# Hybrid SSD and pooling decoder step: the sample's state addition on GpSimd instead of VectorE, and its square sums two pool products later

## The reference

```python
def step(s, inp):                      # per sample token: decay the state, add the outer product
    dec, st = inp
    return s * dec[..., None, None] + st, s
...
y = y_diag + y_off                     # y_t = S_t C_t for the sample
y = y + d_skip * xs
y = y * silu(z)
yg = yg * rsqrt(mean(yg * yg) + EPS)   # per group of 512 channels
...
merged = sigmoid(ga) * (ya @ w_ssd_proj) + sigmoid(gb) * yb
```

## Time and profile before

| | |
|---|---|
| median of 3 runs | 1269.02 us (1268.47 to 1270.06) |
| the profiled execution's own time | 1268.4 us |
| its span, first to last instruction | 1266.7 us |
| mean granted TensorE clock | 0.988 of full speed |
| TensorE busy | 1219.1 us, 96% of the span |
| VectorE busy | 768.0 us, 61% |
| ScalarE busy | 502.7 us, 40% |
| GpSimd busy | 178.5 us, 14% |
| VectorE's 16 state additions (L1376) | 1206 / 1215 / 2934 ns at least, median, most |

### The profile page before, as it was taken

How to read it: one execution, slowest core, us unless ns; L and a number is a source line. 1 busy time by engine, 2 the same in 40 slices (tenths; PEclk the granted TensorE clock), 3 DMA queues, 4 the chain that set the end, 5 groups by cost and what they waited for, 6 DMA issues and landing times.

```text
span 1266.7 us, 22333 instructions
## 1 busy us (share of the span) xinstructions
PE 1219.1 (96%) x9227; PEld 1144.3 (90%) x9227; DVE 768.0 (61%) x1189; ACT 502.7 (40%) x901; POOL 178.5 (14%) x200
## 2 busy tenths in 40 slices
PE   6999999999999999899999998899999999999995
PEld 5999999998888998899999987589999999999995
DVE  5677885467888989943445357434654644644534
ACT  5444544444454577422244234334422422422322
POOL 1000006455002565210010000002000000000000
PEclk7999999999999999999999999999999999999998
DMA  6423223222222876343236258813233223322321
GB/s 230 110 83 90 76 72 101 71 67 67 67 67 63 259 231 183 100 168 100 85 116 238 95 169 268 295 34 102 82 101 100 69 98 100 99 80 86 100 67 68
DMA packets 141339, 147.63 MB, mean 117 GB/s; under 512 B 6339, under 2 KB 134515, under 8 KB 140946
## 3 DMA queue, kind: packets, MB, share of 16 engines
q1 hardware_dynamic: 119124, 126.98, 31.1%
q10 hardware_dynamic: 20224, 8.76, 2.6%
q0 software_dynamic: 1904, 10.65, 2.2%
HBM read 130.35 MB, written 16.68 MB: 116 GB/s over the span
## 4 chain that ended last, share of the span: by engine, by line
PE 77%; DVE 6%; issue 1%; ACT 1%; DVEq 0%; ACTq 0%
PE slot L422 33%; PE slot L440 9%; PE slot L442 5%; PE slot L441 5%; PE slot L439 5%; PE slot L443 5%; PE slot L2017 2%; PE aux L1812 2%; PE aux L2091 1%; PE aux L1804 1%; DVE w_lo L407 1%; PE slot L2112 1%; PE slot L1953 1%; PE aux L1803 1%; DVE outer L1384 1%
## 5 line engine op out<-in xcount | busy, mean ns | idle before, releaser
L407 DVE TENSOR_TENSOR w_lo<-w_raw,w_hi 128x1024 fp32r<-128x1024 f32 x186 | 235.5, 1266 | 313.9 <-ACT w_hi L400 311.4
L400 ACT ACTIVATE w_hi<-w_raw 128x1024 fp32r<-128x1024 f32 x186 | 197.0, 1059 | 475.8 <-PE slot L443 217.1
L422 PE MATMUL slot<-a_hi,w_hi 128*128 128x260 f32 x1392 | 292.0, 291 | 0.0
L422 PE MATMUL slot<-a_hi,w_lo 128*128 128x260 f32 x1392 | 280.4, 283 | 0.0
L422 PE MATMUL slot<-a_lo,w_hi 128*128 128x260 f32 x1392 | 279.8, 283 | 0.0
L422 PEld LDWEIGHTS slot<-a_hi,w_hi 128*128 128x128 f32 x1392 | 216.7, 189 | 12.1 <-issue 11.1
L422 PEld LDWEIGHTS slot<-a_hi,w_lo 128*128 128x128 f32 x1392 | 214.5, 188 | 0.0
L422 PEld LDWEIGHTS slot<-a_lo,w_hi 128*128 128x128 f32 x1392 | 214.5, 188 | 0.0
L440 PE MATMUL slot<-c_two,w_hi 128*128 128x512 f32 x256 | 100.9, 394 | 0.0
L440 PE MATMUL slot<-b_two,w_hi 128*128 128x512 f32 x256 | 100.9, 394 | 0.0
L439 PE MATMUL slot<-b_two,w_hi 128*128 128x264 f32 x256 | 72.9, 285 | 0.0
(11 more groups left out here) (403 smaller groups left out, 2293.3 us busy)
## 6 DMA issues: line engine op xcount, KB each, us to landing
w_raw<-in_w_in SPq DMA_DIRECT2D x32, 1024.0 KB, 5.8
w_raw<-in_w_up SPq DMA_DIRECT2D x16, 1024.0 KB, 5.5
w_raw<-in_w_down SPq DMA_DIRECT2D x16, 1024.0 KB, 5.1
sring<-in_state_ssm SPq DMA_DIRECT2D x16, 512.0 KB, 4.5
out_ssm_sample<-sring ACTq DMA_DIRECT2D x16, 512.0 KB, 4.6
w_raw<-in_w_ssd_proj SPq DMA_DIRECT2D x8, 1024.0 KB, 5.2
cache<-in_cache_mem_k SPq DMA_DIRECT2D x8, 1024.0 KB, 7.7
cache<-in_cache_mem_v SPq DMA_DIRECT2D x8, 1024.0 KB, 6.2
```

Of the source, the lines that this page charges most:

```text
L400: nc.scalar.activation(w_hi[:, t % 2], w_raw[:, t // 2 % 2, :, t % 2 * P:t % 2 * P + P], ACT.Copy).then_inc(hi_ready, 1)
L407: nc.vector.tensor_tensor(w_lo[:, t % 2], w_raw[:, t // 2 % 2, :, t % 2 * P:t % 2 * P + P], w_hi[:, t % 2].bitcast(F32), ALU.subtract).the ...
L422: last = nc.tensor.matmul(slot[t % 2][:, h, 0:HALF], w[:, t % 2, k, :], act[:, k, h * HALF:(h + 1) * HALF], start=(start and k == 0 and n ...
```

## The change

- `update_s` on VectorE becomes `update_state` on GpSimd: the same addition, the same two waits, the same signal. In GpSimd's queue add(0) stands behind decay 1, add(1) behind the store of the prompt's state (L628), and each further add(n) behind decay n+1, ahead of the quad or the pool_lo subtractions of that place. add(15) stands ahead of the last two pool_lo subtractions.
- VectorE's turn loses the addition; `read_s` still waits for `st_new`.
- On TensorE the sum of the sample's squares and its two waits move from ahead of the third pool product to ahead of the fifth. On VectorE its evacuation moves behind the third gated product.

```diff
+            def update_state(n):
+                S = sring[ring(n)]
+                pool.wait_ge(st_dec, n + 1)
+                pool.wait_ge(outer_ready, n + 1)
+                nc.gpsimd.tensor_tensor(S[:], S[:], outer[n][:], ALU.add).then_inc(st_new, 1)
...
             decay_state(0)
             decay_state(1)
+            update_state(0)
             pool.wait_ge(end_ev, 5)
             pool.dma_start(o["ssm_prompt"][0, 0].rearrange("(t h) p n -> (h p) t n", h=2), state_out[:]).then_inc(out_ssm, 16)
+            update_state(1)
             decay_state(2)
             pool.wait_ge(end_ev, 7)
...
             for n in range(3, 16):
                 decay_state(n)
+                update_state(n - 1)
                 if n in (7, 8, 9, 10):
                     add_quad(n - 7)
...
+            update_state(15)
             pool_lo_part(6)
             pool_lo_part(7)
...
-            def update_s(n):
-                S = sring[ring(n)]
-                dve.wait_ge(st_dec, n + 1)
-                dve.wait_ge(outer_ready, n + 1)
-                nc.vector.tensor_tensor(S[:], S[:], outer[n][:], ALU.add).then_inc(st_new, 1)
...
                 for f in TURN_END.get(k - 1, ()):
                     gate_y(f)
-                update_s(k)
                 for f in TURN_MID.get(k, ()):
                     gate_y(f)
                 read_s(k)
...
             pool_gated(1)
+            y_lo(2, a_hi, a_lo)
+            pool_gated(2)
             dve.wait_ge(ys_mm, 1)
             nc.vector.tensor_reduce(y_std[:], aux[:, 0, 0:P].rearrange("p (g k b) -> p g b k", g=GROUPS, b=NS), AX.X,
                                     ALU.add).then_inc(ys_sum, 1)
-            y_lo(2, a_hi, a_lo)
-            pool_gated(2)
...
-                if n == 2:
+                if n == 4:
                     pe.wait_ge(bc_used, 16)
                     pe.wait_ge(ys_sq, 1)
                     nc.tensor.matmul(aux[:, 0, 0:P], ones[:], y_sq[:].rearrange("p k b -> p (k b)"), start=True,
                                      stop=True).then_inc(ys_mm, 1)
```

## The result

The changed kernel takes **1289.03 us** (median of 5 runs, 1288.38 to 1291.45) against 1269.02 (1268.47 to 1270.06) before: 1.0157 times as long, interval 1.0144 to 1.0170. The forecast was 1280, the range 1272 to 1288. The direction was right; the time lies 9 us above the forecast and 1 us outside the range. The profiled execution took 1288.38 us, span 1286.6, which is 19.9 more than the span before.

A forecast was written before the change was run, and what follows sets the result against it. TensorE was taken to set the gate stage's pace, without reserve. Terms 2.5 + 4.6 + 1.4 + 1.2 - 0.4 + 1.8 = 11.1 us on 1268.4 gave 1279.5, forecast as 1280 us; range 1272 to 1288.

The forecast's parts named there:

- The price of an addition: One 128x1024 addition of two full operands takes 2.35 us on GpSimd, against 1.22 on VectorE.
- The near price: Rival: GpSimd adds in 1.91 us, as it multiplies; the loss is 7.5 us, giving 1276 us; chance 0.12.
- Turns 0 to 2: First three gate tiles: add(1) stands behind the prompt's state store on GpSimd; TensorE's first y turn starts 2.5 us late.
- Turn 3: Gate tile 3: y gating waits behind w_lo(4), held until mult(4) and add(3) end; TensorE's y turn costs 4.6 us more.
- the 2.8 case: At gate tile 3's y turn: if w_lo(4) slipped in ahead of add(3), the price would be 2.8 us.
- The clock: Lower granted TensorE clock after the new wait at gate tile 3: 1.8 us added, bounds 0 and 4.5.
- Turn 10: Gate tile 10: the inverse root TensorE wants, queued on VectorE behind read(10), costs 1.4 us through the late add(10).
- Turn 13: Gate tile 13: y scaling for the last inverse roots, behind read(13) on VectorE, costs TensorE 1.2 us.
- The tail: From 513.72 us to the first gated pool product VectorE bounds; saving add(15) gives -0.4 us, bounds -1.2 to +0.7.
- Queues and backlog: State stores, loads and weight units behind the later additions: costed at nothing, as TensorE is late by then too.
- The rival with GpSimd as the bound of turns 7 to 10: At gate tiles 7 to 10 GpSimd needs 9.3 against 7.35 us each; 6 us more, 1286 us; chance 0.15.

The follow-up runs named there:

- reciprocals first: Changed kernel with the reciprocals for y_rows ahead of read(10) and read(11) on VectorE: 1285.06 us.
- the run with the sums back: Changed kernel with the square sums back ahead of the third pool product, additions still on GpSimd: 1286.28 us.
- the run with the sums moved alone: Kernel before with only the square sums moved behind four pool products, additions on VectorE: 1270.31 us.
- the order mended: Changed kernel with add(1), add(2) earlier, reciprocals before read(10), read(11), adds 13 to 15 on VectorE, gated pool products before the sample's y_s sums: 1270.44 us.
- VectorE's additions with the same order behind turn 15: Kernel before, all adds on VectorE, three gated pool products and w_lo(17) ahead of the sample's y_s sums, square sums behind six products: 1265.48 us.

## Why the prediction was right and wrong

- **The price of an addition: right.** Forecast 2.35, measured 2.33 to 2.41 us where it runs alone. The estimate from the Trainium skill's page (GPSIMD Engine Reference, section Elementwise — side-by-side cycle accounting) was 2.39; the trace agrees. The near price falls with it.
- **Turns 0 to 2: right.** 2.5 forecast, 2.86 measured (2.65 from the first state transpose), and by the cause named: with add(1) and add(2) ahead of the stores' waits it goes.
- **Turn 3: the step that failed.** "w_lo(4) runs from there", behind mult(4) and add(3), gave 4.6; it was 7.09. The step took it that VectorE goes between two GpSimd instructions when it has waited through one, as it does in six other places of the changed kernel. In place of that mult(5) and add(4) went first as well, 4.2 us (432.76 against 428.56, the end of add(3), which had been forecast at 428.33). The stand grew by less, because TensorE itself came 1.8 us later than forecast, by turn 2 and the clock behind it. Letting w_lo(4) in front of add(3), the 2.8 case, was worth 8 us of median, 5.9 of them up to the first y_rows. What makes GpSimd win three times there stays open.
- **The clock: the term that was mis-sized.** "The new wait in turn 3 is as long, so I add 1.8 for it; bounds are 0 and 4.5." Behind that wait it was 1.71; but the stands of 1.63 and 1.23 us in turn 2 cost 1.42, the 1.94 in turn 10 cost 1.5, and behind the 4.20 at the third pool product 0.9 more were lost than before. Together 5.5 us, above the upper bound. With the run of reciprocals first, the wait of turn 10 and the low clock behind it went together; in the run with the sums back the wait stayed and the clock did not fall, so a part of this sum is chance.
- **Turn 10: right.** 1.4 forecast, 1.75 measured, and gone with the reciprocals ahead of read(10). **Turn 13: right**, 1.2 against 1.16.
- **The tail: right up to the third product, too small behind it.** Forecast -0.4; -0.1 up to the third product. Behind it 2.6 us came. 0.9 of them are clock; the other 1.65 are the moved square sums, which the forecast had within the bounds, with "about 0.2 us between products": the matmul did cost 0.25, but the gated products behind it came 1.4 later, as in the run with the sums moved alone.
- **Queues and backlog: right to leave out.** The lag is 13.08 us at the end of turn 3 and 13.05 at the end of turn 10, so neither loads nor quads added to it. The rival with GpSimd as the bound of turns 7 to 10 came nearer in time, 1286, but not in place.

The sum: by places, 2.5 us too little in turn 3, 3.7 in the clock (1.42 + 1.71 + 1.5 + 0.9 against 1.8), 1.65 from the moved sums and 1.0 in turns 2, 10, 13 and ahead of the third product make the 8.8 us between 11.1 and 19.9.

## What to carry to other kernels

When work moves to an idle engine, follow that engine's queue instruction by instruction: what the moved work stands behind decides, not how busy the engine is. Here 15 us of VectorE's busy time were saved and 20 us lost at five places; with the order mended and three additions left on VectorE, 2.7 us of loss remained against VectorE's additions with the same order behind turn 15. Where TensorE has no reserve, allow for a lower clock behind every stand, not only the longest, though it did not come behind each; and on engines that exclude each other, bound a wait by all that the other has ready, not by one instruction.

## What the runs showed of the hardware

- **GpSimd can keep VectorE off for several instructions.** w_lo(4) took 7.02, 7.01, 7.02 and 7.04 us in four kernels, behind three GpSimd instructions without a gap, and 5.21 behind two. Elsewhere in the same kernels VectorE gets in after one, and GpSimd's next takes about 1 us longer (2.90 for 1.90). A gap of 0.74 us in which GpSimd waited was enough to let it in. The Trainium skill (SBUF — State Buffer, section SBUF: two separate sides) says that the engine that starts first has the shared ports for its whole instruction and the other blocks; the trace agrees for one instruction, and shows that the next may go first again. What decides it isn't shown.
- **It touches small instructions as well.** With add(1) and add(2) ahead, four instructions of 128x16 took 3.14 us instead of 0.43, through GpSimd's issue of two stores and a multiplication, and one of 128x64 took 1.21 instead of 0.20 beside the end of an addition.
- **The clock fell after some stands of 1.9 us and not after others.** Window 480:500 has 0.91 behind 1.94 us; behind the 2.30 us at 521.12 the window 520:540 has 1.00, and so has 500:520 behind the 1.97 us at 496.90 with the sums back. What the engine did before differs, and no run here tells that apart.
